# Interleaving the first two tiles' input products in a two-layer encoder kernel

## What is computed

```python
h = rms_norm(x, norm_mix[l])
proj = jnp.einsum('bsd,de->bse', h, w_in[l])        # 2048 x 1024 by 1024 x 2048
q_a, k_a, v_a, u_b, q_c, k_c, v_c, g_c = jnp.split(proj, IN_SPLITS, axis=-1)
...
mix = jnp.concatenate([y_a, y_b, y_c], axis=-1)     # attention, pooling, retention
x = x + jnp.einsum('bse,ed->bsd', mix, w_out[l])
x = x + moe_ffn(rms_norm(x, norm_ffn[l]), router_w, router_b, w_gate[l], w_up[l], w_down[l])
```

## Time and profile before

| | us |
|---|---|
| median of 3 runs | 3119.22 (3118.78 to 3120.26) |
| the profiled execution | 3099.97 |
| its span, first to last instruction | 3098.1 |
| TensorE busy | 3046.5 (98%) |
| VectorE, ScalarE, GpSimd busy | 1401.7, 614.2, 1057.3 |

### The profile page before, as it was taken

How to read it: one execution, slowest core, us unless ns; L and a number is a source line. 1 busy time by engine, 2 the same in 40 slices (tenths; PEclk the granted TensorE clock), 3 DMA queues, 4 the chain that set the end, 5 groups by cost and what they waited for, 6 DMA issues and landing times.

```text
span 3098.1 us, 54787 instructions
## 1 busy us (share of the span) xinstructions
PE 3046.5 (98%) x18148; PEld 2176.8 (70%) x18148; DVE 1401.7 (45%) x4048; ACT 614.2 (20%) x1922; POOL 1057.3 (34%) x1250
## 2 busy tenths in 40 slices
PE   8999999999999999999999999999999999999998
PEld 4555555555799999888855555555557999998886
DVE  5576677667322222211155766676673222221111
ACT  1322322322111111101123223223221111111101
POOL 1232132133255555423112232232232555553322
PEclk9999999999999999999999999999999999999999
DMA  8656656653689999999965557656536989999996
GB/s 310 257 187 244 234 193 236 238 187 120 251 292 306 313 313 334 342 353 350 328 247 192 196 218 251 210 208 249 191 131 235 303 296 317 332 328 345 347 354 214
DMA packets 248184, 817.11 MB, mean 264 GB/s; under 512 B 68016, under 2 KB 121264, under 8 KB 188720
## 3 DMA queue, kind: packets, MB, share of 16 engines
q1 hardware_dynamic: 200912, 734.26, 64.1%
q0 software_dynamic: 46112, 77.70, 10.7%
q10 hardware_dynamic: 864, 1.47, 0.2%
HBM read 718.87 MB, written 95.56 MB: 263 GB/s over the span
## 4 chain that ended last, share of the span: by engine, by line
PE 93%; DVE 2%; issue 1%; ACT 1%; DVEq 1%; DMA 1%; another core or an unknown queue 1%; POOL 0%; ACTq 0%; SPq 0%; POOLq 0%
PE bank L2082 31%; PE bank L1785 19%; PE bank L1850 14%; PE bank L2122 9%; PE bank L2112 7%; PE bank L1756 5%; PE bank L1706 2%; PE bank L1936 1%; PE bank L1977 1%; PE bank L2011 1%; DMA arena<-in_x 1%; PE bank L1711 1%; PE bank L1861 1%; PE bank L1945 0%
## 5 line engine op out<-in xcount | busy, mean ns | idle before, releaser
L2082 PEld LDWEIGHTS bank<-arena,wts 128*128 128x128 f32 x8192 | 987.8, 191 | 28.6 <-issue 25.9
L2082 PE MATMUL bank<-arena,wts 128*128 128x128 f32 (+7 forms) x8192 | 998.5, 283 | 9.0 <-issue 8.5
L1785 PE MATMUL bank<-wts 128*128 128x512 f32 x1056 | 469.5, 597 | 0.0
L1850 PE MATMUL bank<-wts,arena 128*128 128x512 f32 x1024 | 455.4, 597 | 1.6 <-ACT arena L1053 1.6
L1681 DVE TENSOR_TENSOR arena<-arena,bank 128x128 f32<-128x128 f32 (+6 forms) x64 | 19.2, 299 | 924.8 <-ACT arena L1115 913.3
L1785 PEld LDWEIGHTS bank<-wts 128*128 128x128 f32 x1056 | 195.0, 190 | 219.7 <-issue 218.1
L828 POOL DMA_INDIRECT arena<-hrows,arena x288 | 291.6, 1012 | 167.7 <-issue 155.5
L1850 PEld LDWEIGHTS bank<-wts,arena 128*128 128x128 f32 x1024 | 190.1, 191 | 217.3 <-issue 214.9
L724 POOL TENSOR_TENSOR arena<-arena 128x256 f32<-128x256 f32 x32 | 25.4, 795 | 861.1 <-DVEq L1417 861.1
L853 POOL DMA_INDIRECT out<-arena x176 | 275.1, 1563 | 54.8 <-issue 54.8
L2122 PE MATMUL bank<-arena,wts 128*128 128x135 f32 (+6 forms) x2176 | 280.0, 289 | 0.0
(11 more groups left out here) (266 smaller groups left out, 3156.5 us busy)
## 6 DMA issues: line engine op xcount, KB each, us to landing
wts<-in_w_gate SPq DMA_DIRECT2D x128, 1024.0 KB
wts<-in_w_up SPq DMA_DIRECT2D x128, 1024.0 KB
wts<-in_w_down SPq DMA_DIRECT2D x128, 1024.0 KB
wts<-wt SPq DMA_DIRECT2D x96, 1024.0 KB, 6.2
wts<-in_w_in SPq DMA_DIRECT2D x88, 1024.0 KB, 7.4
hrows<-arena SPq DMA_DIRECT2D x36, 512.0 KB, 6.2
out<-arena SPq DMA_DIRECT2D x36, 512.0 KB, 3.3
wt<-arena SPq DMA_DIRECT2D x16, 1024.0 KB, 4.2
```

Source lines behind the costliest of these rows:

```text
L1785: i = mm(bIP[j in (1, 3, 6)][:, :], own[:, d], ring[k % SLOTS][:, d], start=(d == 0 and j in (0, 1, 3)), stop=(d == 3), skip_group_check=True)
L1850: i = mm(bIP[k][:, :], dT[o][:, d - 4] if d in (4, 5) else mixT[:, d], wout[:, d, 512 * k:512 * k + 512], start=(n == 0), stop=(n == DC - 1))
L2082: return mm(gu_at(f, k, w), lhs, xT[:, d, 0:w], start=start, stop=(d == DC - 1), skip_group_check=True)
```

## The change

The eight whole products of tiles 0 and 1 keep their operands and banks, and their order becomes (0,0), (0,1), (1,0), (1,1), (0,2), (0,3), (1,2), (1,3), where it was (0,0) to (0,3) and then (1,0) to (1,3). The counts in `whole_prod` and `whole_out` and the bank waits follow. On TensorE `sumsq(1)` now stands behind `whole(0,0)` (before: behind `whole(0,1)`), `sumsq(2)` behind `whole(1,1)` (before: behind `whole(1,0)`). On ScalarE `sumsq_front(1)` goes ahead of the first eviction, and `sumsq_front(2)` stands behind the eviction of (1,1) (before: behind that of (0,3)). The folds stand behind the sixth product as before. The programs of SyncE, VectorE and GpSimd keep their text.

```diff
--- before.py
+++ after.py
@@ -381,11 +381,11 @@
 
         def whole_prod(l, t, n):
 
-            return l * PRODS + (4 * t + n + 1 if t < WHOLE else PRODS - 3 + n)
+            return l * PRODS + (4 * (n // 2) + 2 * t + n % 2 + 1 if t < 2 else 4 * t + n + 1 if t < WHOLE else PRODS - 3 + n)
 
         def whole_out(l, t, n):
 
-            return l * ACT_OUTS + (4 * t + n + 1 if t < WHOLE else ACT_OUTS - 3 + n)
+            return l * ACT_OUTS + (4 * (n // 2) + 2 * t + n % 2 + 1 if t < 2 else 4 * t + n + 1 if t < WHOLE else ACT_OUTS - 3 + n)
 
         def prod_of(l, s, j):
 
@@ -938,13 +938,13 @@
                     o = 1 - b
                     if s == 0:
                         sumsq_first()
-                        whole_columns(0, 0)
                         sumsq_front(1)
-                        for n in range(1, 4):
-                            whole_columns(0, n)
+                        for t in range(2):
+                            for n in range(2):
+                                whole_columns(t, n)
                         sumsq_front(2)
-                        whole_columns(1, 0)
-                        whole_columns(1, 1)
+                        whole_columns(0, 2)
+                        whole_columns(0, 3)
                         for j in range(2):
                             folded(j)
                         whole_columns(1, 2)
@@ -1734,6 +1734,10 @@
                             if t == TILES - 1:
                                 e.wait_ge(hT_ready, (l + 1) * TILES)
                                 e.wait_ge(x_new, (t0 - 2) * 2 + n % 2 + 1)
+                            elif t == 0 and n >= 2:
+                                e.wait_ge(act_out, whole_out(l, 1, n - 2))
+                            elif t == 1:
+                                e.wait_ge(act_out, whole_out(l, 0, n))
                             elif n >= 2:
                                 e.wait_ge(act_out, whole_out(l, t, n - 2))
                             elif t > 0:
@@ -1901,13 +1905,13 @@
 
                     if s == 0:
                         whole(0, 0)
+                        sumsq(1)
                         whole(0, 1)
-                        sumsq(1)
+                        whole(1, 0)
+                        whole(1, 1)
+                        sumsq(2)
                         whole(0, 2)
                         whole(0, 3)
-                        whole(1, 0)
-                        sumsq(2)
-                        whole(1, 1)
                         fold(0)
                         fold(1)
                         whole(1, 2)
```

## The result

The changed kernel takes 3130.95 us (median of 6 runs, 3129.42 to 3133.89), the kernel before 3119.0 (6 runs, 3117.55 to 3120.31): a ratio of 1.0040, 95% interval 1.0030 to 1.0049. It is slower by 12.0 us; the forecast was 3131.3, or 12.1 slower.

A forecast was written before the change was run, and what follows sets the result against it. TensorE, busy 98%, was taken as the bound. Layer 0's 9.1 us (6.87 + 2.27) and layer 1's 3.0 (0.7 + 2.27) made +12.1, giving 3112.1 profiled and, 19 us higher, 3131.3; range 3128 to 3138 for 8 in 10.

The forecast's parts named there:

- Step A: sumsq(1) ahead of whole(0,1), layer 0: one product fewer done before tile 1's rows arrive, +6.87 us.
- rival 4: Clock rises sooner after layer 0's long wait: −1.6 us, 3129.7; counted inside the forecast's 82%.
- 6.8 us at half clock: Half-speed stretch after layer 0's long wait in the kernel before, put at 3.25 us lost.
- Step B: sumsq(2) right behind whole(1,1), both layers: TensorE waits for one eviction and four squares, 2.27 us each.
- Step C: sumsq(1) right behind whole(0,0), layer 1: a wait for tile 1's last piece and squares, 0.7 us.
- What else moves: Shifted work of VectorE, GpSimd and SyncE, such as qk_sums(0), the rotary step and clearing stores: price 0.
- thin cover of 0.5 us: Layer 1: tile 1 ready at 1578.5, whole(0,1) ends at 1579.0, so whole(1,0) does not wait: 0.
- The delay passes through to the end: No later TensorE wait is on an absolute time, since expert weights are issued on TensorE's own counts.
- The 19 us: Median of the runs over the profiled execution of before, not located in the trace; added as the same difference.
- Rival 1: Clock also falls in the new waits, 3.25 us more each: up to +6.5, 3137.8; 12%.
- Rival 2: Tile 1's rows come in time in layer 0, leaving +5.2 us, 3124.5; 4%.
- Rival 3: Reorder hides a late column chunk 3: landing at 60 would give −5.5 us, 3113.7; 2%.

The follow-up runs named there:

- A alone: Kernel before with only sumsq(1) ahead of whole(0,1) and tile 1's squares ahead of the first eviction: 3103.75 us against 3096.99, ratio 1.0025.
- A without B: Changed kernel with ScalarE's squares of tile 2 moved ahead of the eviction of (1,1): 3104.16 us, +7.2 over before, ratio 1.0023.
- B alone: Kernel before with only sumsq(2) moved right behind whole(0,3), ahead of whole(1,0): 3103.05 us, +6.1, ratio 1.0018.
- the rows first: Changed kernel with column chunk 2 issued behind tile 1's rows in layer 0: 3127.1 us, +9.1 over before, ratio 1.0026.
- the late sums: Changed kernel with sumsq(1) put back behind whole(0,1) on TensorE: 3142.17 us, +24.2 over before, ratio 1.0075.
- the warm kernel: Changed kernel with 48 small products in layer 0's long wait for tile 1's rows: 3135.99 us, +18.0 over before.

## Why the prediction was right, point by point

**Step A** was put at +6.87, with the clock's part at 0 and as low as −1.6. Alone it measured +6.8. In the pair of profiles from one group, before first and changed second, the changed kernel resumed 0.4 us earlier and lost 0.65 us less to the clock:

```profile
32.55 23.64 PE L1756 MATMUL bank<-wts,arena 128*128 128x512 f32 x48
32.10 22.99 PE L1760 MATMUL bank<-wts,arena 128*128 128x512 f32 x48
```

That is the direction of rival 4, and so A and B together gave 8.1 there, where 9.1 was put down. But it is no fixed gain of the new order: three profiles of before resume between 31.7 and 32.3, and with A alone the loss to the clock was 2.8 us, with A without B 2.75, hardly less than the 2.8 to 3.05 of before. Two slips in the prediction changed nothing in the sum. Its upper bound for A's clock (3.25 more, so 10.1) did not enter the range, which has 8 without a source. And of the "6.8 us at half clock" some 0.7 lay in the wait itself; 6.1 lay in the product, worth 3.05.

**Step B** was put at 2.27 in each layer, and the waits are 2.27 and 2.27 in one profile, 2.27 and 2.28 in the other. Taking it away from the changed kernel brought about 4.5 us (+7.2 instead of +11.7, across two groups). Missing in this step is a term for the clock. Counting the waits of 2.27 to 2.37 us at L1810 and its like in the profiles of the changed kernel (twice), B alone, the rows first, the late sums and the warm kernel, the clock fell in 6 of 12 and cost 1.6 us each time. On average that is 1.6 us for the two layers. The sum missed it and was some 1 us too high elsewhere, so that its +12.1 lies within 0.4 us of both measurements (+12.0, +11.7) is in part luck; their intervals reach 3 to 5 us to either side.

**Step C** was put at 0.7 and measured 0, 0.66, 0.85, 0.42, 0.59 and 1.17 where it could occur, and 0 with A alone. It follows how late SyncE issues tile 1's rows: the first piece is issued 0.7 us behind the start of `whole(0,0)` where there is no wait, and 1.3 to 1.8 us behind it where the wait is 0.42 to 0.85. From there to ScalarE's first square it is 4.4 us in all of these. Only in the warm kernel, with the 1.17, are the four issues drawn out (3.0 us for 1.75) and that time is 5.4.

**What else moves** was put at 0, and TensorE shows no new wait outside `sumsq(1)` and `sumsq(2)`. The thin cover of 0.5 us at `whole(1,0)` in layer 1 held. GpSimd's rotary step and copies ran from 65.9 to 79.7 us, and TensorE came to their result at 91; tile 2's transposed rows were ready at 65.5, where about 68.5 was forecast. The rest of the mixing took 730.5 to 730.9 us in most profiles of either kernel; in the two of 732.1 and 733.0 the clock had fallen at the end of the steps of layer 0. "The delay passes through to the end" held too: in the pair from one level the two steps 0 grew by 12.8 us together, and the span by 11.2.

**The 19 us** are where the prediction had least to say. It added them as an unexplained constant. They are about 10 us in each expert phase, in which TensorE waits longer and oftener among an expert's gate and up products, and they come with the group of runs and not with the kernel. Adding a constant was right only because the timed runs of both kernels stood at the same level. A comparison of the two first profiles by their spans would have given +30.

**The rivals.** Rival 1 (the clock falls in the new waits) is half true: it does in some, at half the price given. The argument against it placed 2.27 us nearer to the waits of 1.3 us without a fall than to the fall after 4.1. That was a guess from two rows, and the change's own profile has a fall 2.4 us after TensorE became idle. Rival 2 (the rows come in time when timed) is excluded by step A alone at full price; with the rows actually made earlier and B repaired, the new order still cost 5.8 us over the old order with the same loads. Rival 3 (chunk 3 late) has nothing for it: no profile shows a wait for chunk 3.

## What to carry to other kernels

When an order of products is changed, ask first which small step in between needs something that arrives at a fixed time, and count how many products are left to do ahead of it: each one fewer is paid in full. Then look at each small exchange between engines (evict, square, sum) for the product that used to cover it. And before two profiles are compared by their spans, compare a stage that the change cannot touch.

## What was unexpected of the hardware

The granted clock can fall to 1.2 GHz in a wait of 2.3 us and in the next execution not. It fell in or right behind 6 of 12 such waits, for 1.6 us each. After the wait in layer 0 the loss was 3.05, 2.9 and 2.8 us in three profiles of before, 2.8 with A alone, and 2.1, 2.1, 1.5, 2.75 and 2.7 in five of the new order. The Trainium skill says of the slow matmuls at a kernel's start that "it's run-variable" ("TensorE: Matmul & The Clock Gate", "What's actually happening"). It speaks of the start and not of a later wait; these numbers vary in the same way.

The same kernel stands at two levels, 3097 and 3118 us, by the group of runs: 3097 and 3098 on chips 13 and 12, 3118 on chip 15. The difference lies in the expert phases (about 754 and 762 us against 765 and 773), where weights stream in all the time. From 100 to 700 us behind the start of the first of these phases, the transfers ran at 328 to 330 GB/s in all nine profiles of the lower level and at 322 to 324 in all five of the higher. Whether the slower transfers are the cause or follow from the waits isn't shown. Each group had one chip and one time, so whether the level belongs to the chip was not separated, and what differs there was not found out.

The last piece of 128 KB behind three chunks of 2 MB in the queue took 16.9 us to land; with one chunk taken from ahead of it ScalarE had it 5.2 us earlier, and in layer 1, where those chunks had been loaded before, it took 3.1 at most.
